# One layer on one core: the first weight chunk on ScalarE's queue, later chunks behind a wait, and empty products on TensorE

## What is computed

```python
def reference(x, ln_mix_g, w_in, ...):
    h = rmsnorm(x, ln_mix_g[l])
    proj = h @ w_in[l]                       # 1024 -> 5888 columns
    qa, ka, va, qb, kb, vb, ga, gb = jnp.split(proj, splits, axis=-1)
    ...                                      # rotary embedding of q and k
    o_a = moba_attention(qa, ka, va)
    o_b = dilated_attention(qb, kb, vb)
    mix = (jax.nn.sigmoid(ga + b_gate_a[l]) * (o_a @ w_o_a[l])
           + jax.nn.sigmoid(gb + b_gate_b[l]) * (o_b @ w_o_b[l]))
    x = x + mix @ w_out[l]
    h = rmsnorm(x, ln_ffn_g[l])
    x = x + moe_ffn(h, w_router[l], ..., w_gate[l], w_up[l], w_down[l], ...)
    return rmsnorm(x, ln_final_g)
```

## Time and profile before

| | us |
|---|---|
| median of 3 runs | 1143.46 |
| lowest and highest | 1143.41, 1144.5 |
| the profiled execution | 1142.92 |
| its span in the profile | 1141.0 |

### The profile page before, as it was taken

The page is one execution under the profiler, slowest core; times in us unless marked ns, Lnnn a source line. Parts: engine busy times, 40 slices in busy tenths (PEclk is TensorE's granted clock), DMA queues, the critical chain, the costliest instruction groups (busy, mean ns, idle before and its releaser), DMA issues.

```text
span 1141.0 us, 12116 instructions
## 1 busy us (share of the span) xinstructions
PE 1079.2 (95%) x5231; PEld 499.3 (44%) x5231; DVE 306.2 (27%) x689; ACT 214.6 (19%) x368; POOL 3.6 (0%) x11
## 2 busy tenths in 40 slices
PE   7999999999999999999999999999999899999997
PEld 6888889733333333333333333333333333333332
DVE  7566778411111111112111211111111111111112
ACT  5345556211111111111111111101111111110002
POOL 0000000000000000000000000000000000000000
PEclk9999999999999999999999999999999999999999
DMA  9754229999999999999999999999999999999995
GB/s 353 265 177 156 111 80 408 399 393 430 427 428 427 428 428 426 429 426 428 426 428 427 428 427 427 429 427 427 428 428 426 427 429 427 427 430 426 427 430 234
DMA packets 44858, 439.53 MB, mean 385 GB/s; under 512 B 3946, under 2 KB 5506, under 8 KB 20228
## 3 DMA queue, kind: packets, MB, share of 16 engines
q1 hardware_dynamic: 44788, 438.74, 92.1%
q10 hardware_dynamic: 16, 0.00, 0.0%
HBM read 437.68 MB, written 1.05 MB: 385 GB/s over the span
## 4 chain that ended last, share of the span: by engine, by line
PE 67%; DMA 28%; DVE 2%; issue 2%; ACT 1%; POOL 0%; DVEq 0%; ACTq 0%; POOLq 0%
PE ps L1039 40%; DMA pool<-in_w_up_dram 20%; PE ps L694 4%; DMA pool<-in_w_down_dram 4%; DMA attn<-in_w_up_dram 4%; PE ps L1061 4%; PE ps L974 3%; PE ps L724 2%; PE ps L774 2%; PE ps L732 2%; PE ps L1022 1%; PE ps L827 1%; PE ps L828 1%; PE ps L829 1%; DVE w_lo L1206 1%
## 5 line engine op out<-in xcount | busy, mean ns | idle before, releaser
L1039 PE MATMUL ps<-pool,o_t 128*64 128x512 f32 x2144 | 482.4, 596 | 30.4 <-DMA pool<-in_w_gate_dram 11.5
L1039 PEld LDWEIGHTS ps<-pool,o_t 128*64 128x64 f32 x2144 | 153.7, 137 | 317.6 <-issue 275.6
L1477 DVE TENSOR_SCALAR v_tok<-ps 128x512 f32<-128x512 f32 x32 | 22.1, 691 | 503.0 <-PE ps L1039 503.0
L1039 PE MATMUL ps<-attn,o_t 128*64 128x512 f32 x320 | 72.5, 594 | 4.3 <-DMA attn<-in_w_gate_dram 3.5
L628 ACT ACTIVATE o_t<-ps 128x512 f32<-128x512 f32 x32 | 19.1, 597 | 305.1 <-PE ps L694 305.0
L635 ACT ACTIVATE attn<-ps 64x512 f32<-64x512 f32 x60 | 35.5, 591 | 217.1 <-PE ps L1039 216.4
L1039 PE MATMUL ps<-slot_gt,o_t 128*64 128x512 f32 x304 | 69.4, 598 | 4.6 <-issue 2.2
L1039 PE MATMUL ps<-slot_wv,o_t 128*64 128x512 f32 x304 | 69.4, 598 | 4.3 <-issue 2.2
L615 ACT ACTIVATE attn<-v_tok 128x512 f32<-128x512 f32 x32 | 20.2, 630 | 242.1 <-DVE v_tok L1477 242.1
L1061 PE MATMUL ps<-attn,o_t 128*128 128x512 f32 x128 | 60.3, 594 | 0.8 <-DVE attn L1549 0.8
L974 PE MATMUL ps<-xs,work 128*64 128x512 f32 x256 | 60.7, 593 | 0.0
(11 more groups left out here) (195 smaller groups left out, 962.7 us busy)
## 6 DMA issues: line engine op xcount, KB each, us to landing
pool<-in_w_gate_dram SPq DMA_DIRECT2D x45, 2048.0 KB, 37.6
pool<-in_w_up_dram SPq DMA_DIRECT2D x45, 2048.0 KB, 38.2
pool<-in_w_down_dram SPq DMA_DIRECT2D x44, 2048.0 KB, 38.0
attn<-in_w_gate_dram SPq DMA_DIRECT2D x7, 2048.0 KB, 38.1
slot_wv<-in_w_up_dram SPq DMA_DIRECT2D x7, 2048.0 KB, 35.7
slot_gt<-in_w_down_dram SPq DMA_DIRECT2D x7, 2048.0 KB, 42.9
slot_gt<-in_w_up_dram SPq DMA_DIRECT2D x6, 2048.0 KB, 32.9
attn<-in_w_down_dram SPq DMA_DIRECT2D x6, 2048.0 KB, 36.8
```

The costliest lines, as they stand in the source:

```text
L1039: mm = pe.matmul(ps[SLOTS * h:SLOTS * h + SLOTS, bank, :], lhs[:, k, :], ring[n % RING][:, r, 512 * h:512 * h + 512], start=(k == 0 and no ...
L1477: dve.tensor_scalar(g_act, ps[:, G, :], LIMIT, None, ALU.min).then_inc(g_ready, 1)
```

## The change

Four edits:

- The four quarters of chunk 0 are issued by ScalarE's queue, behind its load of the norm weights, and no longer by SyncE's.
- SyncE's queue waits for the first half of x (`ld_x[0]`) after the issue of the identity, and issues the remaining tables and chunks 1 to 3 only then.
- VectorE clears 256 columns of `gates` as its first instruction and signals `zeroed`.
- TensorE runs seven empty products (`run_empty`): float32, 128x256, zeros by zeros, into a bank of `ps` that nothing reads. Five stand ahead of its wait for the identity, one ahead of `turn_input(0)`, one ahead of `turn_input(1)`.

```diff
-            for q in range(PARTS):
-                sp.dma_start(slots[0][:, 2 * q:2 * q + 2, :], win_v[:, 2 * q:2 * q + 2, 0:CHUNK]).then_inc(ld_first[q], 16)
+            sp.wait_ge(ld_x[0], 16)
             sp.dma_start(cst[:, P:N_CONST], consts[:, P:N_CONST]).then_inc(ld_tables, 16)
             for c in range(1, 4):
                 chunk(c)
...
             act.dma_start(rows[0:8, :], row_v[0]).then_inc(ld_mix, 16)
+            for q in range(PARTS):
+                act.dma_start(slots[0][:, 2 * q:2 * q + 2, :], win_v[:, 2 * q:2 * q + 2, 0:CHUNK]).then_inc(ld_first[q], 16)
...
+            def run_empty(count):
+
+                for _ in range(count):
+                    pe.matmul(ps[:, 7, 0:SEQ], gates[:, 0, 0, 0:P], gates[:, 0, 0, :], start=True, stop=True)
+
+            pe.wait_ge(zeroed, 1)
+            run_empty(5)
             pe.wait_ge(ld_cst, 16)
             pe.wait_ge(ld_mix, 16)
             turn(ps[:, 6, 0:8], rows[0:8, :]).then_inc(rows_turned, 1)
...
+            run_empty(1)
             turn_input(0)
+            run_empty(1)
             turn_input(1)
...
+            dve.memset(gates[:, 0, 0, :], 0.0).then_inc(zeroed, 1)
             dve.wait_ge(ld_x[0], 16)
```

More of the change, by code:

```diff
@@ L260, in layer @@
         sq_done, var_ready, rstd_ready, xn_ready = sem("sq_done"), sem("var_ready"), sem("rstd_ready"), sem("xn_ready")
-        neg_half = sem("neg_half")
+        neg_half, zeroed = sem("neg_half"), sem("zeroed")
         rows_turned, cols_ready = sem("rows_turned"), sem("cols_ready")
```

## The result

| | before | with the change |
|---|---|---|
| median, 19 runs each, us | 1143.89 | 1145.55 |
| lowest and highest, us | 1143.07, 1145.49 | 1144.59, 1149.39 |
| ratio, 95% interval | | 1.0015 [1.0009, 1.0022] |
| the profiled execution, us | 1142.92 | 1145.21 |
| its span, us | 1141.0 | 1143.4 |

The change makes the kernel 1.7 us slower, 0.15%. The interval of the ratio excludes 1 and reaches the 0.2% that the prediction set as its bound of "no change".

What follows compares the result with a forecast made beforehand. TensorE's front part, which starts the DMA-full weight stream, was taken as the bound. Low clock gave +2.3 us, full clock +1.7; +2.1 was taken onto 1143.46, giving 1145.6 us, range 1142.7 to 1147.4.

Steps and rivals of the forecast that it cites:

- no change: Whole kernel: a measurement was said to tell 0.2%, 2.3 us, from no change; chance of same 0.58.
- the case with the larger weight: TensorE's start at low clock: late identity and slow turns put chunk 0's products at 13.3 us against 11.01, +2.3 us.
- What bounds the kernel: TensorE's front part starts the weight stream; any shift at chunk 1's first product, 21.92 us, moves the end equally.
- The last quarter: Chunk 0's last quarter shares DMA with tables and chunk 1; copied by 15.1 to 15.9 us, +1.3 to +2.1 us.
- x and identity: Loads sharing DMA with the quarters: x's halves at 5.5 and 7.4 us, identity at 8.6 us.
- If they alternate piece by piece, 1.5 times: DMA engines alternating pieces of x and quarters: x's bytes left after 2.3 us take 1.5 times as long.
- The empties: TensorE warm-up: 0.215 us each at full clock, 0.43 at half; alone between -1.4 and +0.43 us.
- The rule on transposes: Skill's rule that turns do not raise TensorE's clock would gain some 3.7 us more; judged contradicted by the trace.
- The cap on the gain: At chunk 1, ScalarE's copies limit any TensorE gain to at most 1.0 us.
- Sharing by bytes: Rival: DMA engines give ScalarE's queue half the bytes, identity at 10.2 us; +3.2 us, 1146.7 us; chance 0.27.
- x passes ahead, the clock is up: Rival: x ahead of the quarters, turns end at 9.2 to 9.6 us; gain capped at 1.0, 1142.5 us; chance 0.14.
- Nothing moves: Rival: x ahead but clock low, or clock gain offset by the late quarter; 1143.9 us; chance 0.15.

Runs made afterwards that it cites:

- Experiment 9: The kernel before with twelve empty products between the products of chunk 0 and chunk 1, a pure TensorE delay; ratio 1.0048 [1.0034, 1.0061].
- experiments 3: The change without SyncE's wait for x, so tables and chunk 1 are issued earlier; ratio 1.0025 [1.0015, 1.0035] against the kernel before.
- experiment 4: The change with SyncE held until the third quarter of chunk 0 instead of x's first half; ratio 0.9998 [0.9989, 1.0007] against the kernel before.
- experiment 7: The change without empties, SyncE issuing x only after ScalarE's first small load, so behind the quarters; ran once, 1146.53 us.
- experiment 1: The change without its seven empty products, queue move and hold kept; ratio 1.0016 [1.0007, 1.0025] against the kernel before.
- experiment 5: The change without empties and with SyncE held until the third quarter of chunk 0; ratio 1.0003 [0.9994, 1.0013] against the kernel before.
- experiment 2: The kernel before with the seven empties and the clearing, quarters on SyncE's queue, no hold; ratio 0.9989 [0.9980, 0.9998].
- experiments 11 and 12: The kernel before with nine empties ahead of the identity, none later; then also four low-by-high products ahead of the last quarter's; both 0.9996 [0.9987, 1.0005].

## Why the prediction came out

**The forecast.** 1145.6 us was predicted and 1145.55 measured; a shift of +2.1 us against the median of the three runs shown (1143.46) and of +1.7 in the timed comparison, whose runs of before have their median at 1143.89. The closeness is partly luck: the case with the larger weight, a bound by identity and turns at +2.3 us, did not occur (the products of chunk 0 began 1.2 us later than before, not 2.3), and the one that did came out larger than its own sum.

**What bounds the kernel.** Right. Chunk 1's first product was named as the place behind which nothing is absorbed, and +2.28 us there became +2.27 at the first piece of the ring and +2.38 at the last one. Experiment 9 shows it with a delay of known size. That the last two agree so well is luck, since the stream alone differs by up to 2 us between executions.

**The last quarter.** Right in mechanism: sharing with tables and chunk 1 at half pace (2.64 us predicted for a quarter, 2.8 measured). It is the bound in the trace, and experiments 3 and 4 move it both ways. Its size, the last copy of chunk 0 ready at 15.1 to 15.9 us (15.69), came out by errors that offset each other. The prediction had 2.3 to 2.6 quarters left at 7.9 us, because it counted sixteen pieces on each engine for each half of x, where its own working a paragraph earlier has eight; with eight at least 2.5 would have been left. In the trace 1.9 quarters (1.01 of 2.10 MB) were left at 8 us. Against that, the sum had no time between the last bytes (near 13.75) and the copy (14.63), 0.9 us here. At TensorE it was +2.28, just above the +1.3 to +2.1 of the sum, since the four products behind the wait took 0.28 us more than a quarter of sixteen.

**x and identity.** Wrong, as a step: "If they alternate piece by piece, 1.5 times" from 2.3 us on. The first half of x was not delayed at all, because the quarters' bytes did not flow from 2.3 us but from 4 to 5 (experiment 7). The timeline of the changed kernel on VectorE:

```profile
4.51 1.22 DVE L1176 CUSTOM_DVE_ANT_0 work<-xs 128x1024 f32<-128x1024 f32 x1 [3.40 <-DMA xs<-in_x_dram]
```

4.51 against 4.45 before. The second half came 0.7 us late in this trace (6.46) and not in experiment 1's (5.84). The identity was predicted at 8.6 and came at 7.47, 7.19 to 7.53 in the other kernels with the move and x ahead, against 5.89 to 6.70 where the quarters are on SyncE's queue (and no empties stand in front of it). The rule of the Trainium skill ("DMA: Bandwidth & Descriptors", Queues, rings and completion order), that the engines go round between queues by packets, had led the prediction to 4.5 us for the first half of x, and that is when it came. But x did not pass by taking turns: the quarters were not flowing yet. Where both flow, the trace agrees with turns by packets and not by bytes (217 to 202 in experiment 7); how many pieces make one turn it does not show.

**The empties.** Two terms were off. I read the four products of the earlier trace rows as four whole f32 products of 512 columns. The trace of the change counts ten instructions for its five first empties (1.17 us, x10) and 4.29 us. So an f32 product is two instructions here, and an empty costs 0.86 us at the lower clock and 0.43 at the upper (24 instructions in 5.34 us in experiment 9), twice the terms in the sum. The other term was the clock. I kept both a low and a high one; the change had first the one, then the other. The granted clock in the profile's rows reads 1.00 from 1 us on, also where the empties ran at 0.43 us an instruction, so it does not show the rise; the pace does. Nine of the ten instructions of the first five empties have the lower pace and the last one, from 5.0 us, the upper. The fall is in the rows (busy columns, then clock, DMA share, GB/s):

```profile
8.50:11.80 3.30, 3.30 (x16) 3.01 (x15) 2.28 (x5) 1.26 (x2) 0.00 (x0) 0.50 1.05 390
```

The clock was up at about 5 us, after nearly 4 us of empties, and near 8.5 us, in the middle of the first half's turns, it is back at 0.50 (1.2 GHz), after TensorE had stood idle for 2.0 us before the identity and worked for 1.0. It returns with the first products of chunk 0, near 11.8. The turns thus began at the upper clock and ended at the lower one, and the empty between their halves cost 0.86 us. In the sum this was hidden: products would have begun at 11.93 us and then waited for the last quarter anyway. Once the quarter is in time it is not hidden in the trace (experiment 4, +1.05), though the time shows no loss there that is clear of noise.

**The rule on transposes.** The trace of before contradicted the rule of the Trainium skill ("TensorE: Matmul & The Clock Gate", Part 4) that turning does not bring the clock up. The experiments without empties repeat it: in experiment 5 sixteen turns in 3.59 us, no product ahead, and then sixteen products at the upper pace (3.93 us busy).

**The cap on the gain.** I put it at 1.0 us, by chunk 1's copies. The real one is nearer: VectorE's `h_hi` of the second half, 0.3 us. I had looked at TensorE's and ScalarE's waits, and VectorE had none in the start of before because TensorE was always later.

**The rivals.** Sharing by bytes falls with experiment 7: the load that is issued first passes first, and when both flow they share by packets, with twice the bytes for x. "x passes ahead, the clock is up" was half true, and its gain was stopped by the late quarter, as the reason against it said; without the quarter it is 0.3 us (experiment 2), not 1.0. "Nothing moves" falls: chunk 1 moved by 2.28 us and the interval of the ratio excludes 1, though by the bound of 0.2% the two kernels are not told apart.

## What to carry to other kernels

Two transfers on two queues share the same DMA engines, so a load moved to another queue to be early takes its bytes from the next load; lay out which piece is needed last, and hold the other queue until that piece is nearly through; here 3 to 3.5 us passed between the issue and its effect. Before shortening a stage, look for the engine that has no waits there only because the one in front of it was slow: here VectorE had 0.3 us of slack and ate a gain of 0.95. TensorE warmed up by empty products stayed at the upper clock over two gaps of 0.6 us (experiment 2), but not over one of 2.0 us (the change).

## What the runs showed of the hardware

- On empty DMA engines bytes flow about 1 us after the issue (x: issued at 0.72, first packets between 1.5 and 1.75 us in before). With another queue's load in front it was 2.8 to 3.6 us, in both directions: x behind quarters, quarters behind x, tables behind quarters. About 1 MB passes on the first queue meanwhile. After that both queues pass about as many packets: 373 to 401 packets in 4 us where both have pieces of about 2 KB, and a quarter of 512 KB takes 2.8 us instead of 1.3; 217 to 202 in 3 us, with twice the bytes for x, where its pieces are twice as long.
- The same turns and first products met TensorE's upper clock at different points: the sixteen products of chunk 0 took 4.06 us in one execution of before and 5.01 with a hold that changed nothing that TensorE waits for, and chunk 1's first product stood at 22.06 and 23.07 us. The same five empties took 4.29 us in the change, with the last instruction at the upper clock, and 4.63 in experiment 4, all at the lower; there the turns behind them began at the lower clock too. Nine took 6.65 and 5.69 us (experiments 11 and 12). In the change the upper clock was gone again 3 us after the empties, 2 us of them idle. A warm-up of one length does not serve every execution.
- With full DMA engines the same stream of weights took up to 1.9 us more from one execution to another, over some 950 us, whatever the edits at the start.
